# Five linear layers of a two-block transformer started two tiles at a time, with a chunked scratch layout and two gate buffers

## The chip, the cores and the metric

The kernel runs on one core of a Trainium2 chip, in one launch. The metric is the device time of that core in microseconds (us). Engines are called PE (matrix multiply), DVE (vector), ACT (activations), POOL (the general engine) and SP (which here only issues DMAs).

## What is computed

Two blocks on a sequence of 1024 tokens with 1024 features, in float32.

First block, once:

```python
h = h + hybrid_mixer(rmsnorm(h), ...)      # projection, gate z, conv, state space scan in 8 chunks of 128, pooling
h = h + memory_cross_attention(rmsnorm(h), rmsnorm(mem), ...)
h = h + swiglu(rmsnorm(h), ...)
x = rmsnorm(h)
```

In the state space part (16 heads of 64, 2 groups, state 128) each chunk of 128 tokens needs the running sum `a_cs` of every head along the tokens, spread over all partitions, for `exp(a_cs[l] - a_cs[s])`. The result is multiplied by `silu(z)`, z being the first 1024 columns of the input projection.

Second block, two layers: an even one (`proj` into a grouped attention with 8 heads, a latent attention with 8 heads, and a gate of 1024 columns), and an odd one (windowed attention with 16 heads and a sink, and a gate). Each is

```python
h = rms_norm(x, norm_w) * (1 + scale) + shift
y = (attention(h @ w_in) * silu(gate)) @ w_out
x = x + gate_mod * y
```

and a last `rms_norm`.

## The kernel before, in words

Activations lie with the features on the partitions: eight blocks k of 128 features by 1024 tokens. Every product is made of three: each float32 operand is split into a high half, rounded by ACT (`wh`, `XH`, `AH`, `RAWH`), and a low half, the rest, made by DVE (`wl`, `XL`, `AL`, `RAWL`). `pe_linear` (L280 to L308) is the linear layer: for each tile j of 128 output columns it runs over the eight k and issues six matmuls of 128x512 for each (three products, two halves of the tokens), which accumulate in one of four PSUM tiles `P` of 128x1024. In tile 0 it waits for block k by `ready(k)` just before that block's six matmuls; later tiles need no wait. A function in `between` runs on PE after the tile of that number.

Weights come by one list, `order`, of slabs of 1024x128 (512 KB). `sp_weights` (L230) loads slab i into `wf[i % 2]` once slab i-2's low half is made. `act_weights` (L242) rounds it into `wh[i % 2]` once PE has ended the tile of slab i-2; `dve_weights` (L251) makes `wl`. So the weights of tile 2 are split when tile 0 has ended. ACT and DVE do this at the head of their work on each tile (`act_tiles`, `dve_tiles`), and every engine works through its program in the order written.

A root mean square norm over the features goes: squares by ACT (L348), sums by DVE (L355), `pe_roots` (16 matmuls of one column, L364), the square root on ACT (L371), five short DVE steps and a diagonal (L394), `pe_spread` (4 matmuls, L402), and the copy out by ACT (L408).

The five layers that matter here:

- `z0`, five tiles of the gate z, at the start. ACT and DVE make the halves of block k of the raw input in turn. The roots of the first norm run after tile 0 and its spread after tile 1; DVE and ACT can start on the gate and on x1 only after that spread.
- `lq`, two tiles, at the start of the even layer. After tile 0 PE runs the spread `d1`. ACT copies it out, DVE scales the eight blocks of H by it (L1728), SP writes each to DRAM (`spill2`, L678), and only then issues the load of the weight slab of layer `ck` (L239). ACT's next weight split stands in its program ahead of the second tile's square, which the norm of `lq` needs.
- `eo`, eight tiles, the even layer's output. Blocks 0 to 3 of the attention result are gated already. For blocks 4 to 7 ACT makes the silu (L2370), DVE multiplies (L2327), ACT rounds (L2372), DVE makes the low half (L1300), one block after the other.
- `vo`, two tiles, at the start of the odd layer. DVE and ACT make the shifted norm block by block (L1697, L1687, L1701).
- `oo`, eight tiles, the odd layer's output. For each block DVE multiplies by the gate (L2727), ACT rounds (L2714), DVE makes the low half (L1300). The gates lie in four buffers `T`; gate j of 4 to 7 is loaded by SP when the low half of block j-4 is there (L2558).

The state space part: after the convolution layer, layer `z2` makes the last two gate tiles. `act_conv`'s `gate` (L727) puts silu of the tile in the one buffer `ZG` (L733) and ACT issues the store to `scratch_g` (L735); the second waits until the first store has landed. ACT's split of the weights of `so`, the layer after the scan, stands ahead of each of the two gates. PE's first transposes of the scan wait until both gates have left PSUM. ACT writes the running sums `[16 heads, 1024]` to the DRAM tensor `scratch_a` (L869). `sp_rows(n)` (L878) loads the 128 columns of chunk n from it, spread over all 128 partitions, 1 MB in SBUF: for each partition 16 pieces of 512 bytes, 4 KB apart in DRAM. SP issues chunks 0 to 3 in `sp_conv` after the weights of `z2`, chunk 4 and the gates' loads (L931) after `z2`, chunks 5 and 6 during the scan, and chunk 7 after the eight reloads of H. `act_decay(n)` (L1045, L1050) works on chunk n.

Of the kernel before, what the change touches and what calls it, by code (L numbers as in the profile page):

```python
# [7 lines left out]
F32 = mybir.dt.float32  # L8
# [111 lines left out]
class Kernel:  # L120
# [159 lines left out]
    def pe_linear(self, e, stage, xh, xl, ready, emptied, tokens=S, width=128, between=None, through=()):  # L280

        j = 0
        for n in range(self.count[stage][0]):
# [177 lines left out]
    def pe_z0(self, e):  # L461
# [4 lines left out]
                       lambda j: [(self.s.dve, ("z", j))], between=between)  # L466
# [225 lines left out]
    def act_conv(self, e):  # L692
# [34 lines left out]
        def gate(e, j):  # L727
            e.wait_ge(*self.s.mm.to(("z2", j)))
            if j:
                e.wait_ge(*self.s.g[6].to("out"))  # L730
            else:
                e.wait_ge(*self.s.act.to("dtx"))
            e.activation(sb["ZG"][:, :], self.tile("z2", j), ACT.Silu).then_inc(*self.s.act.up(("z", 6 + j)))  # L733
            e.wait_ge(*self.s.act.here())
            e.dma_start(self.dr["gT"][:, 6 + j, :], sb["ZG"][:, :]).then_inc(*self.s.g[6 + j].up("out"))  # L735
        self.act_tiles(e, "z2", gate)
# [26 lines left out]
    def sp_conv(self, e):  # L763
# [8 lines left out]
        self.sp_weights(e, self.no["so", 0])  # L772
        e.wait_ge(*self.s.dt.to("rows"))
        self.sp_rows(e, 0)
        self.sp_rows(e, 1)
# [86 lines left out]
    def act_dt_sums(self, e):  # L862
# [6 lines left out]
        e.dma_start(self.dr["aT"], rows).then_inc(*self.s.dt.up("rows"))  # L869
# [7 lines left out]
    def sp_rows(self, e, n):  # L877
        e.dma_start(self.rows_of(n)[:, :, :],  # L878
                    self.dr["aT"][:, 128 * n:128 * n + 128].partition_broadcast(128)).then_inc(*self.s.r[self.ROWS[n]].up(n))
# [207 lines left out]
    def dve_ssd(self, e):  # L1087
# [21 lines left out]
        for c in range(-1, 8):  # L1109
# [15 lines left out]
            if c > 0:  # L1125
# [3 lines left out]
                else:  # L1129
                    e.wait_ge(*s.g[7].to("out"))  # L1130
# [744 lines left out]
    def pe_even(self, e):  # L1875
        s = self.s

        def linear(stage, emptied, behind=None):
            self.pe_linear(e, stage, self.XH, self.XL, self.x4_ready, emptied, between=behind and {0: behind})
# [480 lines left out]
    def pe_even_out(self, e):  # L2360
        s = self.s
        self.pe_linear(e, "eo", self.AH, self.AL, lambda k: [(s.lo, ("eo", k))], lambda j: [(s.dve, ("h5", j))])
# [18 lines left out]
    def dve_even_out(self, e):  # L2381
        s = self.s
        for j in range(8):
            if j > 3:
                self.dve_gate(e, j)
# [27 lines left out]
    def pe_odd(self, e):  # L2413
        s = self.s
        ready = lambda k: [(s.lo, ("x5", k))]
        self.pe_linear(e, "vo", self.XH, self.XL, ready, lambda j: [(s.act, ("vo", j))])
# [288 lines left out]
    def pe_odd_out(self, e):  # L2705
        s = self.s
        self.pe_linear(e, "oo", self.XH, self.XL, lambda k: [(s.lo, ("oo", k))], lambda j: [(s.dve, ("h6", j))])
# [369 lines left out]
```

## Time and profile before

| | |
|---|---|
| median of 3 runs | 3194.72 us (3190.4 to 3196.64) |
| the profiled execution: its time | 3196.34 us |
| its span in the profile | 3194.5 us |
| PE busy | 2965.2 us, 93% of the span |
| DVE, ACT, POOL busy | 1694.7, 1262.5, 386.0 us |
| mean granted clock of PE | 0.967 of full speed |

The time of the execution is 1.84 us longer than the span, which is what lies around it. Matmul records overlap, since a matmul is pipelined: the start of one to the start of the next is what PE spends on it.

### The profile page before, as it was taken

The numbers are of one execution on the slowest core, as the hardware profiler recorded it, in microseconds if no ns is written. First come the engines' busy times: TensorE is split into PE (matmuls) and PEld (weight loads), VectorE is DVE, ScalarE is ACT, GpSimd is POOL, SyncE is SP. The second block draws the span as 40 slices with busy tenths as digits, with TensorE's granted clock in tenths as the row PEclk, the third lists the DMA queues.
The fourth block names the chain that finished last, engine by engine and source line by source line (L and its number), as shares of the span: only waits on it lengthen the run. The fifth ranks groups of instructions, "written<-read, shape, count | busy, mean of one in ns | idle before, by whom it ended". The sixth has DMA issues, their size and how long they took to land.

```text
span 3194.5 us, 38728 instructions
## 1 busy us (share of the span) xinstructions
PE 2965.2 (93%) x15570; PEld 2481.8 (78%) x15570; DVE 1694.7 (53%) x2101; ACT 1262.5 (40%) x2078; POOL 386.0 (12%) x224
## 2 busy tenths in 40 slices
PE   8999987899999999999999789889999889999987
PEld 6877865688988777888888567778888667879965
DVE  6563555654454444444344625688888634326653
ACT  5321445322343111111112325577767524427741
POOL 0000004200000000000000000255445100004410
PEclk9999998999999999999999899999999989999988
DMA  4112245112302222332331211100001221121031
GB/s 138 53 47 100 67 98 159 41 33 75 98 21 60 79 84 83 86 90 73 87 89 45 97 43 60 53 1 11 11 14 55 85 92 40 56 87 43 16 106 66
DMA packets 244528, 210.99 MB, mean 66 GB/s; under 512 B 9072, under 2 KB 219120, under 8 KB 243840
## 3 DMA queue, kind: packets, MB, share of 16 engines
q1 hardware_dynamic: 240864, 195.88, 20.9%
q10 hardware_dynamic: 3488, 12.65, 1.1%
q8 instruction: 125, 2.05, 0.3%
q14 instruction: 51, 0.42, 0.0%
HBM read 175.93 MB, written 30.47 MB: 65 GB/s over the span
## 4 chain that ended last, share of the span: by engine, by line
PE 81%; DVE 8%; ACT 5%; issue 2%; DMA 2%; POOL 2%; SPq 1%; DVEq 0%; ACTq 0%; POOLq 0%
PE P L300 59%; PE P L269 4%; PE P L2062 3%; PE P L272 2%; PE P L274 2%; PE P L273 2%; POOL T L2322 1%; PE P L2076 1%; DVE PTL L1300 1%; PE P L2075 1%; PE P L943 1%; DVE WST L2301 1%; PE P L402 1%; PE P L1332 1%; PE P L364 1%
## 5 line engine op out<-in xcount | busy, mean ns | idle before, releaser
L256 DVE TENSOR_TENSOR wl<-wf,wh 128x1024 fp32r<-128x1024 f32 (+4 forms) x239 | 251.7, 1053 | 1026.0 <-ACT wh L248 1025.8
L248 ACT ACTIVATE wh<-wf 128x1024 fp32r<-128x1024 f32 (+4 forms) x239 | 220.0, 921 | 1170.2 <-PE P L300 1047.5
L300 PE MATMUL P<-AQ,wh 128*128 128x512 f32 x1920 | 519.8, 393 | 13.1 <-DVE AQ L1300 10.6
L300 PE MATMUL P<-XH,wh 128*128 128x512 f32 (+1 forms) x1376 | 438.0, 400 | 46.1 <-DVE XL L1701 17.1
L2322 POOL TENSOR_TENSOR T<-T,WST 128x1024 f32<-128x1024 f32 x128 | 242.6, 1896 | 1668.9 <-DVE WST L2294 1668.9
L300 PEld LDWEIGHTS P<-AQ,wh 128*128 128x128 f32 x1920 | 362.5, 189 | 91.4 <-issue 10.4
L300 PE MATMUL P<-XL,wh 128*128 128x512 f32 (+1 forms) x1376 | 430.8, 395 | 0.0
L300 PE MATMUL P<-XH,wl 128*128 128x512 f32 (+1 forms) x1376 | 429.9, 394 | 0.0
L300 PEld LDWEIGHTS P<-XH,wh 128*128 128x128 f32 (+1 forms) x1376 | 258.3, 190 | 117.4 <-issue 40.1
L300 PEld LDWEIGHTS P<-XL,wh 128*128 128x128 f32 (+1 forms) x1376 | 260.5, 189 | 58.6
L300 PEld LDWEIGHTS P<-XH,wl 128*128 128x128 f32 (+1 forms) x1376 | 260.1, 189 | 58.1
L300 PE MATMUL P<-AQ,wl 128*128 128x512 f32 x960 | 297.7, 392 | 0.0
L300 PEld LDWEIGHTS P<-AQ,wl 128*128 128x128 f32 x960 | 181.7, 189 | 38.2
L300 PE MATMUL P<-FF,wh 128*128 128x512 f32 x704 | 193.0, 397 | 6.0 <-ACT wh L248 3.0
L1300 DVE TENSOR_TENSOR PTL<-P,PTH 128x512 fp32r<-128x512 f32 x256 | 164.5, 684 | 53.2 <-ACT PTH L2201 52.1
L269 PE MATMUL P<-consts,T 128*128 128x128 f32 x1112 | 146.5, 275 | 28.2 <-POOL T L2322 25.2
L2201 ACT ACTIVATE PTH<-P 128x512 fp32r<-128x512 f32 x256 | 139.1, 595 | 83.5 <-PE P L269 80.8
L300 PEld LDWEIGHTS P<-FF,wh 128*128 128x128 f32 x704 | 134.1, 192 | 36.6 <-ACT wh L248 6.0
L2301 DVE TENSOR_REDUCE WST<-P 128x1 f32<-128x1024 f32 x128 | 155.8, 1217 | 1.7 <-PE P L2062 1.6
L269 PEld LDWEIGHTS P<-consts,T 128*128 128x128 f32 x1112 | 124.3, 141 | 40.6 <-DVE PTL L1300 23.7
L2701 POOL TENSOR_TENSOR WS<-WS,WST 128x768 f32<-128x768 f32 (+1 forms) x64 | 87.3, 1363 | 466.7 <-DVE WST L2680 456.4
L2208 ACT ACTIVATE T<-P,WST 128x1024 f32<-128x1024 f32 x128 | 143.4, 1120 | 0.1
(379 smaller groups left out, 4926.4 us busy)
## 6 DMA issues: line engine op xcount, KB each, us to landing
AW<-ada_w SPq DMA_DIRECT2D x48, 512.0 KB, 3.7
wf<-w_gate_up SPq DMA_DIRECT2D x44, 512.0 KB, 4.9
wf<-w_in SPq DMA_DIRECT2D x28, 512.0 KB, 3.8
scratch_h<-H SPq DMA_DIRECT2D x24, 512.0 KB, 5.7
H<-scratch_h SPq DMA_DIRECT2D x24, 512.0 KB, 7.6
scratch_g<-T ACTq DMA_DIRECT2D x22, 512.0 KB, 3.2
wf<-odd_w_in SPq DMA_DIRECT2D x20, 512.0 KB, 3.7
wf<-even_w_in SPq DMA_DIRECT2D x17, 512.0 KB, 3.8
```

Source lines behind the costliest of these rows:

```text
L248: e.activation(self.sb["wh"][i % 2][:, 0:m], self.sb["wf"][i % 2][:, 0:m], ACT.Copy).then_inc(*self.s.w_hi.up(i))
L256: e.tensor_tensor(l, f, h.bitcast(F32), ALU.subtract).then_inc(*self.s.w_lo.up(i))
L269: return e.transpose(out, in_, self.sb["consts"][p0:p0 + n, a + p0:a + p0 + n])
L272: e.matmul(out, wh, xh, start=first, stop=False)
L300: ins = e.matmul(self.P[slot][0:m, t:t1], w, x[:, k, t:t1], start=first and k == 0, stop=last and k == kb - 1)
L1300: e.tensor_tensor(lo, src, hi.bitcast(F32), ALU.subtract).then_inc(*self.s.lo.up(name))
L2062: ins = e.matmul(p[:, ks], a[:, qs], c[:, ks], start=m == 0, stop=m == len(passes) - 1)
L2201: e.activation(self.probs("PTH", at, d), self.turned(d), ACT.Copy).then_inc(*s.hi.up(("pt", at, d)))
L2208: e.activation(self.px(at), self.P[at % 2], ACT.Exp, bias=w[:, 0:1], accum_out=w[:, 1:2]).then_inc(*s.act.up(("exp", at)))
L2301: e.tensor_reduce(sb["WST"][n % 4][:, 0:1], self.P[n % 2], AX, ALU.max, negate=True).then_inc(*s.dve.up(("max", n)))
L2322: e.tensor_tensor(self.px(n), self.px(n), r, ALU.mult).then_inc(*s.pool.up(("sc", n)))
L2701: e.tensor_tensor(x, x, r, ALU.mult).then_inc(*s.pool.up(("wsc", n)))
```

## The change

- `pe_first_pair` is new: tiles 0 and 1 of a layer are made side by side. For k from 0 to 5 the six matmuls of tile 0 are followed by those of tile 1; then tile 0's k 6 and 7, its signal and its `between`, then tile 1's. Both tiles' weights are waited for ahead of the first matmul. Layers `z0`, `lq`, `eo`, `vo` and `oo` use it.
- In `eo` the silu and the gating of block j+1 are put ahead of the halves of block j, on ACT and on DVE; in `oo` DVE's gating likewise.
- `ZG` becomes two buffers, the second at T + 4096, where the convolution's buffers were; the second gate waits for no store, and the split of a slab of `so` stands behind each gate. What waited for the second store in the scan (a write to T[3]) waits for the first one.
- `scratch_a` becomes `[8, 16, 128]`: the store is cut in pieces of 512 bytes, and the load of a chunk reads, for each partition, 8 KB in a run.
- SP issues the rows of chunk 0 ahead of the weight slabs of `z2`.

```diff
+    def pe_first_pair(self, e, stage, xh, xl, ready, emptied, between):
+        halves, slots = [], []
+        for j in range(2):
+            i = self.no[stage, j]
+            halves.append(tuple(self.halves(i)))
+            slots.append(self.tiles[stage, j][0])
+            e.wait_ge(*self.s.w_hi.to(i))
+            e.wait_ge(*self.s.w_lo.to(i))
+            self.pe_place(e, slots[j])
+        kb = self.order[self.no[stage, 0]].shape[1]
+        steps = [(j, k) for k in range(kb - 2) for j in range(2)] + [(j, k) for j in range(2) for k in (kb - 2, kb - 1)]
+        for j, k in steps:
+            if j == 0:
+                for count, key in ready(k):
+                    e.wait_ge(*count.to(key))
+            w1, w2 = (h[:, k, :] for h in halves[j])
+            for w, x, first, last in ((w1, xh, True, False), (w1, xl, False, False), (w2, xh, False, True)):
+                for t in (0, 512):
+                    ins = e.matmul(self.P[slots[j]][:, t:t + 512], w, x[:, k, t:t + 512], start=first and k == 0,
+                                   stop=last and k == kb - 1)
+            if k == kb - 1:
+                ins.then_inc(*self.s.mm.up((stage, j)))
+                self.emptied[slots[j]] = emptied(j)
+                if between and j in between:
+                    between[j](e)
...
@@ pe_linear
-        j = 0
-        for n in range(self.count[stage][0]):
+        j = 2 if paired else 0
+        if paired:
+            self.pe_first_pair(e, stage, xh, xl, ready, emptied, between)
+        for n in range(j, self.count[stage][0]):
...
@@ act_conv
         def gate(e, j):
             e.wait_ge(*self.s.mm.to(("z2", j)))
-            if j:
-                e.wait_ge(*self.s.g[6].to("out"))
-            else:
+            x = sb["ZG"][j][:, :]
+            if j == 0:
                 e.wait_ge(*self.s.act.to("dtx"))
-            e.activation(sb["ZG"][:, :], self.tile("z2", j), ACT.Silu).then_inc(*self.s.act.up(("z", 6 + j)))
+            e.activation(x, self.tile("z2", j), ACT.Silu).then_inc(*self.s.act.up(("z", 6 + j)))
             e.wait_ge(*self.s.act.here())
-            e.dma_start(self.dr["gT"][:, 6 + j, :], sb["ZG"][:, :]).then_inc(*self.s.g[6 + j].up("out"))
-        self.act_tiles(e, "z2", gate)
+            e.dma_start(self.dr["gT"][:, 6 + j, :], x).then_inc(*self.s.g[6 + j].up("out"))
+            self.act_weights(e, self.no["so", j])
+        for j in range(2):
+            gate(e, j)
@@ sp_conv
-        self.sp_weights(e, self.no["so", 0])
+        self.sp_weights(e, self.no["z2", 0])
         e.wait_ge(*self.s.dt.to("rows"))
         self.sp_rows(e, 0)
+        self.sp_weights(e, self.no["so", 0])
         self.sp_rows(e, 1)
@@ act_dt_sums, sp_rows
-        e.dma_start(self.dr["aT"], rows).then_inc(*self.s.dt.up("rows"))
+        e.dma_start(self.dr["aT"].rearrange("n h t -> h n t"),
+                    rows.rearrange("h (n t) -> h n t", n=8)).then_inc(*self.s.dt.up("rows"))
...
-                    self.dr["aT"][:, 128 * n:128 * n + 128].partition_broadcast(128)).then_inc(*self.s.r[self.ROWS[n]].up(n))
+                    self.dr["aT"][n].partition_broadcast(128)).then_inc(*self.s.r[self.ROWS[n]].up(n))
@@ dve_ssd
-                    e.wait_ge(*s.g[7].to("out"))
+                    e.wait_ge(*s.g[6].to("out"))
@@ act_even_out (dve_even_out has the same shift of dve_gate)
-            if j > 3:
-                e.wait_ge(*s.gl[j].to("back"))
-                e.activation(GA[:, j, :], GA[:, j, :], ACT.Silu).then_inc(*s.act.up(("gate", j)))
+            if 3 <= j < 7:
+                e.wait_ge(*s.gl[j + 1].to("back"))
+                e.activation(GA[:, j + 1, :], GA[:, j + 1, :], ACT.Silu).then_inc(*s.act.up(("gate", j + 1)))
@@ dve_odd_out
-        for j in range(8):
+        def gate(j):
             e.wait_ge(*s.gl[j].to("end"))
             e.tensor_tensor(T[j % 4], self.sb["O2"][j][:, :], T[j % 4], ALU.mult).then_inc(*s.dve.up(("o2", j)))
+        gate(0)
+        for j in range(8):
+            if j < 7:
+                gate(j + 1)
             self.dve_low(e, ("oo", j), self.XL[:, j, :], T[j % 4], self.XH[:, j, :])
...
-    sb["ZG"] = put("ZG", "T", 8256 + 4096, [128, 1024], F32)
+    sb["ZG"] = [put(f"ZG{i}", "T", (8256 + 4096, 4096)[i], [128, 1024], F32) for i in range(2)]
...
-    dr["aT"] = nc.dram_tensor("scratch_a", [16, S], F32, kind="Internal").ap()
+    dr["aT"] = nc.dram_tensor("scratch_a", [8, 16, 128], F32, kind="Internal").ap()
```

## Rows read from the trace of the kernel before

**Rows 1.** The page: busy time of each engine.

```profile
PE 2965.2 (93%) x15570; PEld 2481.8 (78%) x15570; DVE 1694.7 (53%) x2101; ACT 1262.5 (40%) x2078; POOL 386.0 (12%) x224
```

**Rows 2.** Timeline of `z0`: start, us, engine, line, out<-in, count [idle before].

```profile
12.12 2.05 PE L300 MATMUL P<-RAW,wh 128*128 128x512 f32 x4 [12.12 <-DVE RAW L449]
...
16.97 1.07 PE L300 MATMUL P<-RAW,wh 128*128 128x512 f32 x4
...
29.56 1.84 PE L364 MATMUL P<-consts,T 128*128 128x1 f32 x16
...
42.29 1.88 PE L402 MATMUL P<-T,consts 128*128 128x512 f32 x4
...
43.61 1.50 PE L300 MATMUL P<-RAW,wh 128*128 128x512 f32 x4
...
33.53 1.22 DVE L394 TENSOR_TENSOR T<-consts,RS 128x1024 f32<-128x1024 f32 x1
```

**Rows 3.** Timeline of `lq`, PE, DVE, SP and ACT.

```profile
1788.29 1.19 PE L300 MATMUL P<-XH,wh 128*128 128x512 f32 x2 [5.08 <-DVE XL L1701]
...
1806.17 1.88 PE L402 MATMUL P<-T,consts 128*128 128x512 f32 x4
...
1830.21 1.92 PE L364 MATMUL P<-consts,T 128*128 128x1 f32 x16 [0.35 <-DVE T L355]
...
1809.15 9.65 DVE L1728 SCALAR_TENSOR_TENSOR H<-H,vecs,T 128x1024 f32<-128x1024 f32 x8 [0.40 <-ACT T L408]
...
1819.20 13.47 SPq L239 DMA_DIRECT2D wf<-even_w_in  x4
...
1825.83 1.06 ACT L248 ACTIVATE wh<-wf 128x1024 fp32r<-128x1024 f32 x1 [5.96 <-DMA wf<-even_w_in]
```

**Rows 4.** Timeline of `eo`, PE and DVE.

```profile
2514.07 2.05 PE L300 MATMUL P<-AQ,wh 128*128 128x512 f32 x4 [6.38 <-DVE AQ L1300]
...
2542.95 1.07 PE L300 MATMUL P<-AQ,wh 128*128 128x512 f32 x4
...
2544.31 1.07 PE L300 MATMUL P<-AQ,wh 128*128 128x512 f32 x4
...
2523.08 1.23 DVE L1300 TENSOR_TENSOR AQ<-O,AQ 128x1024 fp32r<-128x1024 f32 x1 [1.13 <-ACT AQ L2372]
```

**Rows 5.** Timeline of `vo`, PE.

```profile
2632.22 1.19 PE L300 MATMUL P<-XH,wh 128*128 128x512 f32 x2 [5.03 <-DVE XL L1701]
...
2650.12 0.62 PE L300 MATMUL P<-XH,wh 128*128 128x512 f32 x2
```

**Rows 6.** `oo`: PE's timeline, and the landing time of the gates' loads (L2558).

```profile
3064.25 1.19 PE L300 MATMUL P<-XH,wh 128*128 128x512 f32 x2 [4.56 <-DVE XL L1300]
...
3090.05 0.62 PE L300 MATMUL P<-XH,wh 128*128 128x512 f32 x2
...
DMA to landing us min/median/max: 3.6/3.7/4.3
```

**Rows 7.** Timeline around `z2` and the scan's start, PE and ACT.

```profile
492.28 1.94 PE L269 MATMUL P<-consts,XS 128*128 128x128 f32 x8 [25.72 <-ACT ZG L733]
...
475.23 1.06 ACT L248 ACTIVATE wh<-wf 128x1024 fp32r<-128x1024 f32 x1 [16.84 <-DMA wf<-w_out_mix]
...
491.11 1.02 ACT L733 ACTIVATE ZG<-P 128x1024 f32<-128x1024 f32 x1 [12.38 <-DMA scratch_g<-ZG]
```

**Rows 8.** DMA views: 504 to 517 us, one chunk's rows alone; then 0 to 60.

```profile
DMA packets 2065, 1.07 MB, mean 82 GB/s; under 512 B 16, under 2 KB 2064, under 8 KB 2064
...
GB/s 0 164 328 303 328 407 401 421 412 412 410 360 294 251 7 0 0 0 0 0 0 0 200 159 1 0 0 0 0 0 48 298 277 355 71 0 0 0 0 0
```

**Rows 9.** The last chunk's rows: timeline of ACT, DVE and PE.

```profile
570.25 4.78 ACT L1045 ACTIVATE RM<-RM,AT 128x128 f32<-128x128 f32 x16 [11.17 <-DMA RM<-scratch_a]
...
576.15 2.35 DVE L1097 TENSOR_TENSOR RM<-RM,P 128x1024 f32<-128x1024 f32 x2 [3.08 <-ACT RM L1050]
...
580.82 1.98 PE L989 MATMUL P<-ST,BC 128*128 128x512 f32 x4 [2.84 <-DVE ST L1143]
```

More of the change, by code:

```diff
@@ L278, in tile, with pe_linear @@
         return self.P[slot][0:m, 0:tokens]
-    def pe_linear(self, e, stage, xh, xl, ready, emptied, tokens=S, width=128, between=None, through=()):
-        j = 0
-        for n in range(self.count[stage][0]):
+    def pe_first_pair(self, e, stage, xh, xl, ready, emptied, between):
[23 more added lines that the diff above has]
+                    between[j](e)
+    def pe_linear(self, e, stage, xh, xl, ready, emptied, tokens=S, width=128, between=None, paired=False,
+                  through=()):
+        j = 2 if paired else 0
+        if paired:
+            self.pe_first_pair(e, stage, xh, xl, ready, emptied, between)
+        for n in range(j, self.count[stage][0]):
             i = self.no[stage, n]
@@ L465, in pe_z0 @@
                        lambda k: [(self.s.hi, ("raw", k)), (self.s.lo, ("raw", k))],
-                       lambda j: [(self.s.dve, ("z", j))], between=between)
+                       lambda j: [(self.s.dve, ("z", j))], between=between, paired=True)
     def act_z0(self, e):
@@ L1878, in linear @@
         def linear(stage, emptied, behind=None):
-            self.pe_linear(e, stage, self.XH, self.XL, self.x4_ready, emptied, between=behind and {0: behind})
+            self.pe_linear(e, stage, self.XH, self.XL, self.x4_ready, emptied, between=behind and {0: behind},
+                           paired=stage == "lq")
         linear("lq", lambda j: [(s.act, ("lq", "sq", j))], lambda e: self.pe_spread(e, "d1", self.T[2]))
@@ L2361, in pe_even_out @@
         s = self.s
-        self.pe_linear(e, "eo", self.AH, self.AL, lambda k: [(s.lo, ("eo", k))], lambda j: [(s.dve, ("h5", j))])
+        self.pe_linear(e, "eo", self.AH, self.AL, lambda k: [(s.lo, ("eo", k))], lambda j: [(s.dve, ("h5", j))],
+                       paired=True)
         self.pe_rstd(e, "n5", self.T[2], s.dve.to(("n5", "sum", 7)))
@@ L2383, in dve_even_out @@
         for j in range(8):
-            if j > 3:
-                self.dve_gate(e, j)
+            if 3 <= j < 7:
+                self.dve_gate(e, j + 1)
             self.dve_low(e, ("eo", j), self.AL[:, j, :], self.sb["O"][:, j, :], self.AH[:, j, :])
@@ L2415, in pe_odd @@
         ready = lambda k: [(s.lo, ("x5", k))]
-        self.pe_linear(e, "vo", self.XH, self.XL, ready, lambda j: [(s.act, ("vo", j))])
+        self.pe_linear(e, "vo", self.XH, self.XL, ready, lambda j: [(s.act, ("vo", j))], paired=True)
         self.pe_linear(e, "ko", self.XH, self.XL, ready, lambda j: [(s.act, ("ko", j))])
@@ L2706, in pe_odd_out @@
         s = self.s
-        self.pe_linear(e, "oo", self.XH, self.XL, lambda k: [(s.lo, ("oo", k))], lambda j: [(s.dve, ("h6", j))])
+        self.pe_linear(e, "oo", self.XH, self.XL, lambda k: [(s.lo, ("oo", k))], lambda j: [(s.dve, ("h6", j))],
+                       paired=True)
         self.pe_rstd(e, "n6", self.T[2], s.dve.to(("n6", "sum", 7)))
```

## The prediction, made before the changed kernel was run

> **What bounds the kernel now.** I read the page first: PE is busy for 2965.2 of 3194.5 us [rows 1], so a gain can only come from the 229 us in which PE stands still, or from stretches in which its clock is low. The list of PE's waits was next, then the timeline around each place that the diff touches. The reader is to see two kinds of stall. One is a single large one: PE ends `z2` and then stands for 25.72 us until ACT has copied out the last gate tile [rows 7]. The others lie in tile 0 of a layer whose input is made block by block: PE has six matmuls for a block and then waits for the next. What PE does at full clock is seen in tile 1 of `eo`, where the last two blocks start at 2542.95 and 2544.31 [rows 4]: 1.36 us for a block of six matmuls, so 0.2267 for one, 10.88 for a tile, 21.76 for a pair. After a long idle it is slower: in `z0` the first 12 matmuls took 16.97 - 12.12 = 4.85 us [rows 2] instead of 2.72, mostly at the lower of the clock's two levels (1.2 and 2.4 GHz). So a start costs 2.13 us more, and I charge that to every pair.
>
> **What the pairs do.** Nothing is computed more or less. A pair has 2.72 us of PE work per block where tile 0 had 1.36. DVE makes a block's input in two operations of 1.2 to 1.3 us, less than 2.72 where nothing else holds it, so PE becomes the bound, and the pair ends 21.76 + 2.13 = 23.89 us after its start.
>
> - **`vo`.** Start 2632.22, end 2656.1. Before, tile 1 began at 2650.12 [rows 5] and ended 10.88 later, at 2661.0. Gain 4.9.
> - **`eo`.** Start 2514.07, end 2538.0. Before, tile 1's last block began at 2544.31 [rows 4] and ended at 2545.7. Gain 7.7. This holds if the halves keep up. The low half of a block takes 1.23 us, and DVE stood 1.13 us before it, waiting for ACT [rows 4]: DVE's gating and ACT's rounding of one block ran one after the other. With the gating one block ahead, DVE has two operations of about 1.2 us a block and no wait, 2.35 us, below PE's 2.72.
> - **`oo`.** Start 3064.25, end 3088.1. Before, tile 1 began at 3090.05 [rows 6] and ended at 3100.9. Gain 12.8. It is the largest since tile 0 took 25.8 us here for 48 matmuls. The gating one ahead now stands in DVE's program in front of a low half, so a late gate load would hold the block before it. Load j starts when the low half of j-4 is done, and DVE has four operations, some 4.7 us, before it needs it; it lands in 3.6 to 4.3 us [rows 6]. That is hidden, with 0.4 to spare; if it is not, PE has 0.4 us a block in hand.
> - **`z0`.** Here tile 0 ends later: 84 matmuls (14 blocks) and 2.13 us after 12.12, at 33.3, where it ended at 29.56. The roots run then, and the diagonal was ready 33.53 + 1.22 - 29.56 = 5.19 us after their start [rows 2]. Tile 1's last two blocks (2.72) are too little to cover that, so PE waits for it at 38.5 and the spread of 43.61 - 42.29 = 1.32 us ends at 40.0 instead of 43.61. Everything behind hangs on the spread. Gain 3.6, not the 9 that the pair as such would give.
> - **`lq`.** This one should lose. The spread `d1` stands behind tile 0. It began at 1806.17; now it begins 19.04 + 2.13 us after 1788.29, at 1809.5 [rows 3], 3.3 later. ACT's copy, DVE's eight operations of 9.65 us, SP's spills and, behind them on SP's queue, the slab load issued at 1819.20 all hang on it. ACT then split that slab after a wait of 5.96 us for the load, at 1825.83, and the second square of `lq` stands behind that split, and PE's roots at 1830.21 behind that. Tile 1 ends earlier, but PE only waits longer before the roots. Loss 3.3. Below: 0, if the load is found not to be last. Above: 5, if the roots run at the lower clock after the longer wait.
>
> In all five the weights of tile 2 are split when tile 0 has ended: one ACT operation of 1.06 and one DVE operation of 1.23, 2.3 us with little between, and PE has 2.72 us of tile 1 left. The cover is 0.3 us at most; gone, it costs what is missing, once a layer. I take 0.
>
> **The scan.** ACT's program held the split of the first `so` slab ahead of the gate, and it waited 16.84 us for that slab's load, until 475.23; then the second gate waited 12.38 us for the first one's store, until 491.11 [rows 7]. Both loads and store stood in queues behind the rows of chunks 0 to 3. With two buffers the first gate waits for its tile alone, and the second for the end of `z2`, 492.28 - 25.72 = 466.56 [rows 7]. ACT's 1.02 us and some 0.2 for the two signals give PE's start at 467.8 instead of 492.28. Gain 24.5. PE is then not idle before: its eight transposes took 1.94 us at the lower level [rows 7], half of that at the higher one; gain 1.0, between 0 and 1.9.
>
> This needs the first `so` slab by 466. SP's program now has rows 0 before the slabs of `z2`, some 12 us earlier, and the same rows 1, 2 and 3 before `so`. **The rows' cost** is what the trace does not show in the new form. One chunk alone took some 13 us, 1 MB at 82 GB/s in pieces under 2 KB [rows 8]. Bounds: the same rate, and the 400 to 421 GB/s at which the input's pieces of 4 KB came [rows 8], 2.6 us. I take the fast end, since the new pieces are in one run like those; but all partitions read the same 8 KB, which no row shows, so the slow end stays open. The Trainium skill ("DMA: Bandwidth & Descriptors", Specifications) gives 512 bytes as the least transfer for line rate, and by it the old pieces would be large enough and the new ones no faster; the trace disagrees for the old ones, which ran at a fifth of the rate of the others. By that rule the sum would be the first rival's.
>
> The **last chunk's rows** were late: ACT waited 11.17 us for them, until 570.25, DVE 3.08 for ACT, and PE 2.84 for DVE [rows 9]. They are issued at the same point as before. If they land 6 us earlier, none of these waits is left; gain 2.8, and 0 if the rate is the old one. The store of `scratch_a` in 128 pieces instead of 16 moves 64 KB and has some 12 us until SP reaches it; cost 0. Reading g[6] instead of g[7] takes a wait off DVE that was over anyway; 0. Scan together: 24.5 + 1.0 + 2.8 = 28.3. ACT's decays, which bound the first chunks, only move.
>
> **Sum.** 3.6 + 28.3 - 3.3 + 7.7 + 4.9 + 12.8 = 54.0 us. Between these places PE is the bound, or (in the attention) work that only moves, so the gains add. Against the profiled execution's 3196.34 us this is 3142.3; the median of the runs is 1.6 lower, so I say 3142.
>
> **Rivals.**
> - *The rows are no faster* (12%). For: the same-address reads, and the rule above. Then the last chunk's wait stays, 2.8. If the first `so` slab still lands at 475.2, ACT's second gate stands behind it and PE starts at 477.5, 9.7 later; but rows 0 has left the queue 12 us ahead, which speaks for no such loss. 3145 to 3155, likeliest 3147.
> - *`lq` loses nothing* (8%): the load lands in time whatever the spread does. ACT's 5.96 us wait for it speaks against that. 3139.
> - *The weights of tile 2 are late* (7%), by some 1 us in each of four layers, the cover being 0.3. 3146.
> - *The clock* (3%), the one on the other side. The pair changes the PSUM tile with every six matmuls; if PE does not come to the higher level in it, 12 matmuls cost 4.85 throughout. Then each pair of 96 takes 38.8 instead of 23.9 us, three times 14.9 more, and `z0`'s and `lq`'s 84 take 12.8 more each: 70.3 us, 3212, slower by 17. It decides from 54 us on, that is if about 11 of the 15 us come in each of the five. Against: before, PE rose within 5 us of every steady start. The Trainium skill ("TensorE: Matmul & The Clock Gate", A second HAM failure mode) tells of a kernel whose clock swung since it cycled through PSUM banks with short idles between. No row here shows that for pairs.
> - The forecast itself has 68%, and 2% is left for what I don't see.
>
> **How the numbers follow.** Within the forecast the cold start may cost nothing or twice as much in each pair: 10.7 us either way, 3132 to 3153. The rows' slow end reaches 3155, the `lq` rival lies inside. Range 3131 to 3156. About 0.2% (6 us) is what a measurement of this kernel can tell from no change. Faster has all but the clock and half of the unseen: 0.96; same 0.01; slower 0.03.
>
> **What the new profile would show.** PE's wait for `ZG` near 467 gone or under 2 us; the rows' loads landing in 3 to 5 us; ACT's wait at L1045 gone; in `eo`, `vo` and `oo` no waits of PE for low halves after the first block; in `z0` a wait of about 1 us before the spread; in `lq` a longer wait before the roots. I am wrong if `z0` gains the full 9 us or `lq` gains, if rows land after 12 us, or if the clock column shows low levels inside the pairs.

## The result, and the profile after

The changed kernel takes 3141.61 us (median of 4 runs, 3140.52 to 3146.3), against 3193.23 us (3190.4 to 3196.64) for the kernel before beside it: a ratio of 0.9841, 95% interval 0.9824 to 0.9858, so 51.6 us faster. The forecast said 3142. By the profiled executions it is less close: that of the changed kernel took 3146.3 us, with a span of 3144.5, so the spans differ by 50.0 us where the sum of the forecast had 54.0. That the median fell on the forecast is thus partly luck, and the terms are judged by the traces.

Lines of the changed kernel's code that come up below: L300 is the pair's matmul, L331 that of later tiles, L395 the roots, L433 a spread, L763 the gate's `ZG`, L912 the rows' load, L1079 the decay, L1762 the scaling of x0, L1334 a low half. First the page, and rows of PE's list of waits (who waited for what; us in total, times, longest):

```profile
PE 2956.3 (94%) x15570; PEld 2482.8 (79%) x15570; DVE 1694.3 (54%) x2101; ACT 1261.3 (40%) x2078; POOL 385.7 (12%) x224
```

```profile
PE P L395 <- DVE T L386: 17.3, 3, 7.4
PE P L300 <- DVE RAW L480: 12.2, 1, 12.2
PE P L300 <- DVE XL L1735: 10.1, 2, 5.1
...
PE P L300 <- DVE AQ L1334: 6.4, 1, 6.4
...
PE P L300 <- DVE XL L1334: 4.6, 1, 4.6
...
PE P L269 <- ACT ZG L763: 1.2, 1, 1.2
```

PE's work is the same [rows 1]. L300 is in the pairs alone, and its waits for input are one at each pair's start (1, 2, 1 and 1 times, five in all) and none inside a pair. The wait for the last gate is 1.2 us instead of 25.72 [rows 7]. One wait has grown: the roots, up to 7.4 us at a time.

The gain, stretch by stretch. Each is from one PE row to another in both traces, so the rows add up to the difference of the spans.

| stretch | before | after | gain | forecast |
|---|---|---|---|---|
| start to the first tile behind `z0`'s spread | 43.61 | 40.81 | 2.8 | 3.6 |
| to the end of `z2` | 422.95 | 424.19 | -1.2 | 0 |
| to the first matmul of `so` (the scan) | 128.53 | 100.30 | 28.2 | 28.3 |
| to the first of `lq` | 1193.20 | 1191.12 | 2.1 | 0 |
| to the first behind `lq` and `ck` | 67.23 | 72.78 | -5.6 | -3.3 |
| to the first of `eo` | 658.55 | 659.07 | -0.5 | 0 |
| `eo` to its roots | 103.14 | 95.63 | 7.5 | 7.7 |
| to the first of `vo` | 15.01 | 15.01 | 0.0 | 0 |
| `vo` to the first of `ko` | 28.8 | 23.38 | 5.4 | 4.9 |
| to the first of `oo` | 403.25 | 404.30 | -1.1 | 0 |
| the pair of `oo` | 36.68 | 24.50 | 12.2 | 12.8 |
| to the end of the span | 93.6 | 93.4 | 0.2 | 0 |

**The scan.** ACT's timeline (start, us, line, tile) around the two gates, and PE's first transposes:

```profile
456.74 1.01 ACT L763 ACTIVATE ZG<-P 128x1024 f32<-128x1024 f32 x1
...
458.22 1.06 ACT L248 ACTIVATE wh<-wf 128x1024 fp32r<-128x1024 f32 x1 [0.48 <-ACT ZG L763]
465.04 1.02 ACT L763 ACTIVATE ZG<-P 128x1024 f32<-128x1024 f32 x1 [5.76 <-PE P L331]
...
466.21 1.06 PE L269 MATMUL P<-consts,XS 128*128 128x128 f32 x8 [1.21 <-ACT ZG L763]
```

The split of the `so` slab has no DMA to wait for (16.84 us before), the second gate waits for PE's tile only, and the transposes run at the higher clock, 1.06 us instead of 1.94 [rows 7]. The rows' loads (line L912, DMA view) land in a third of the time; before, the middle one took 17.7 us:

```profile
DMA to landing us min/median/max: 4.4/5.1/8.1
```

**`lq`.** PE, with DVE's and ACT's rows that hold it up:

```profile
1756.42 1.19 PE L300 MATMUL P<-XH,wh 128*128 128x512 f32 x2 [5.08 <-DVE XL L1735]
...
1778.38 1.88 PE L433 MATMUL P<-T,consts 128*128 128x512 f32 x4
...
1801.29 3.54 PE L395 MATMUL P<-consts,T 128*128 128x1 f32 x16 [7.38 <-DVE T L386]
...
1781.36 9.65 DVE L1762 SCALAR_TENSOR_TENSOR H<-H,vecs,T 128x1024 f32<-128x1024 f32 x8 [0.40 <-ACT T L439]
...
1796.92 1.06 ACT L248 ACTIVATE wh<-wf 128x1024 fp32r<-128x1024 f32 x1 [4.84 <-DMA wf<-even_w_in]
```

The spread comes 21.96 us after the first matmul instead of 17.88 [rows 3], 4.1 us later. The slab's load takes part of that back, since ACT waits 4.84 us for it instead of 5.96: the roots start 44.87 us after the first matmul instead of 41.92, 3.0 later. After 7.38 us of idle instead of 0.35 they take 3.54 us instead of 1.92, and the tile behind them, still partly at the lower clock, takes 13.56 us (1804.70 to 1818.26) instead of 12.59 (1831.99 to 1844.58). That is 3.0 + 1.6 + 1.0 = 5.6 us.

**`z0` and `oo`.** In `z0` PE now waits a little for the diagonal, as the forecast had it. In `oo` the pair runs without a stop; DVE waits once for a gate's load, and PE does not notice:

```profile
34.14 1.84 PE L395 MATMUL P<-consts,T 128*128 128x1 f32 x16
...
39.39 1.98 PE L433 MATMUL P<-T,consts 128*128 128x512 f32 x4 [0.53 <-DVE T L425]
40.81 1.49 PE L331 MATMUL P<-RAW,wh 128*128 128x512 f32 x4
...
3026.59 1.19 PE L300 MATMUL P<-XH,wh 128*128 128x512 f32 x2 [4.57 <-DVE XL L1334]
...
3051.09 0.66 PE L331 MATMUL P<-XH,wh 128*128 128x512 f32 x2
...
3039.34 1.22 DVE L2765 TENSOR_TENSOR T<-O,T 128x1024 f32<-128x1024 f32 x1 [1.41 <-DMA T<-scratch_g]
```

### The profile page after: what moved, and what is told of

It is laid out like the page before. It is cut to its first block, busy times and chain, and to the rows that moved or that the text cites. A ratio compares the mean times of both kernels' runs of the same rounds, so it can differ in the third digit from the quotient of the medians.

```text
span 3144.5 us, 38727 instructions
## 1 busy us (share of the span) xinstructions
PE 2956.3 (94%) x15570; PEld 2482.8 (79%) x15570; DVE 1694.3 (54%) x2101; ACT 1261.3 (40%) x2078; POOL 385.7 (12%) x224
## 4 chain that ended last, share of the span: by engine, by line
PE 85%; DVE 6%; ACT 3%; issue 2%; POOL 2%; DMA 1%; SPq 0%; DVEq 0%; ACTq 0%; POOLq 0%
PE P L331 59%; PE P L269 4%; PE P L300 4%; PE P L2097 3%; PE P L272 2%; PE P L274 2%; PE P L273 2%; POOL T L2357 2%; PE P L2111 1%; PE P L977 1%; DVE PTL L1334 1%; PE P L2110 1%; PE P L433 1%; DVE WST L2336 1%; PE P L1366 1%
## 5 line engine op out<-in xcount | busy, mean ns | idle before, releaser
L331 PE MATMUL P<-AQ,wh 128*128 128x512 f32 x1856 | 498.9, 391 | 2.6 <-issue 2.6
L331 PE MATMUL P<-XH,wh 128*128 128x512 f32 (+2 forms) x1280 | 402.2, 396 | 17.3 <-ACT T L379 9.1
L331 PEld LDWEIGHTS P<-AQ,wh 128*128 128x128 f32 x1856 | 348.6, 188 | 76.3 <-issue 4.1
L331 PE MATMUL P<-XL,wh 128*128 128x512 f32 (+2 forms) x1280 | 398.2, 393 | 0.0
L331 PE MATMUL P<-XH,wl 128*128 128x512 f32 (+2 forms) x1280 | 397.7, 392 | 0.0
L331 PEld LDWEIGHTS P<-XH,wh 128*128 128x128 f32 (+2 forms) x1280 | 239.8, 188 | 74.8 <-issue 22.8
L331 PE MATMUL P<-AQ,wl 128*128 128x512 f32 x928 | 286.6, 390 | 0.0
L331 PEld LDWEIGHTS P<-XH,wl 128*128 128x128 f32 (+2 forms) x1280 | 240.5, 188 | 53.5
L331 PEld LDWEIGHTS P<-XL,wh 128*128 128x128 f32 (+2 forms) x1280 | 240.3, 188 | 53.7
L331 PEld LDWEIGHTS P<-AQ,wl 128*128 128x128 f32 x928 | 174.5, 188 | 36.6
L331 PE MATMUL P<-FF,wh 128*128 128x512 f32 x704 | 192.9, 397 | 6.7 <-ACT wh L248 3.6
L1334 DVE TENSOR_TENSOR PTL<-P,PTH 128x512 fp32r<-128x512 f32 x256 | 164.6, 684 | 53.5 <-ACT PTH L2236 52.4
L269 PE MATMUL P<-consts,T 128*128 128x128 f32 x1112 | 146.2, 275 | 28.3 <-POOL T L2357 25.4
L331 PEld LDWEIGHTS P<-FF,wh 128*128 128x128 f32 x704 | 134.2, 192 | 37.4 <-ACT wh L248 6.7
```

Of the source, the lines that this page charges most:

```text
L269: return e.transpose(out, in_, self.sb["consts"][p0:p0 + n, a + p0:a + p0 + n])
L331: ins = e.matmul(self.P[slot][0:m, t:t1], w, x[:, k, t:t1], start=first and k == 0, stop=last and k == kb - 1)
L1334: e.tensor_tensor(lo, src, hi.bitcast(F32), ALU.subtract).then_inc(*self.s.lo.up(name))
```

## Experiments

Ten kernels ran. Each is given with its ratio to the kernel before, run beside it on the same chip (medians 3193.2 to 3198.2 in the four sessions), and with the stretch of the trace that the edit touches. Some 6 us is what a median can tell; the stretches are finer, about 0.1 us where the rows in them have the same clock. Of the variants of the changed kernel all but e5, e7 and e8 lie within 6 us of it, so what is said of them rests on the stretches.

### 1 and 2: which edit emptied the scan's wait?

The forecast gave 24.5 us to the two gate buffers. The rival owner is the scratch layout. Each is put alone into the kernel before.

```diff
e1: kernel before, and only
-        e.dma_start(self.dr["aT"], rows)
+        e.dma_start(self.dr["aT"].rearrange("n h t -> h n t"), rows.rearrange("h (n t) -> h n t", n=8))
...
-        self.dr["aT"][:, 128 * n:128 * n + 128].partition_broadcast(128)
+        self.dr["aT"][n].partition_broadcast(128)
...
-    dr["aT"] = nc.dram_tensor("scratch_a", [16, S], F32, kind="Internal").ap()
+    dr["aT"] = nc.dram_tensor("scratch_a", [8, 16, 128], F32, kind="Internal").ap()
e2: kernel before, and only the change's act_conv gate, ZG in two buffers, and dve_ssd's wait for g[6]
```

> The kernel before with the new layout of the scratch tensor and nothing else: one gate buffer, the old order on ACT and SP, no pairs. Theory (the clogged queue is the cause): a chunk's rows land in about 5 us instead of 14 to 28, so the first slab of so is there before ACT asks for it and the store of the first gate lands in about 4 us, before z2 ends. The stall of 25.7 us ahead of the scan falls under 2 us and the last chunk's wait of 11 us is gone: some 28 us faster than the kernel before, about 3165, without a second buffer. Rival (the single buffer is the cause, as my forecast told it): the second gate still waits several us for the store; a gain of 2.8 us for the last chunk and part of the 24.5.

> The kernel before with two gate buffers and the split of the so slabs behind each gate, but the old layout, the old order of SP, no pairs. Theory (the clogged queue): ACT's split of the first so slab still waits for the load until about 475, now behind the first gate and ahead of the second, so the second gate comes at about 476 and PE starts the scan at about 477.5 instead of 492.3: 12 to 15 us faster, 3179 to 3182, and the last chunk's wait of 11 us on ACT stays. Rival (the buffer alone frees it): PE starts at 468 and the kernel is 24 us faster, about 3170.

Layout alone: 3165.41 us, ratio 0.9904 (0.9890 to 0.9919). Buffers alone: 3180.44 us, 0.9952 (0.9937 to 0.9966). First the timeline of the kernel with the layout alone, ACT and PE:

```profile
460.43 1.04 ACT L248 ACTIVATE wh<-wf 128x1024 fp32r<-128x1024 f32 x1
461.38 1.01 ACT L733 ACTIVATE ZG<-P 128x1024 f32<-128x1024 f32 x1
...
469.77 1.00 ACT L733 ACTIVATE ZG<-P 128x1024 f32<-128x1024 f32 x1
...
470.92 1.07 PE L269 MATMUL P<-consts,XS 128*128 128x128 f32 x8 [2.21 <-ACT ZG L733]
```

And with the buffers alone:

```profile
457.87 1.01 ACT L732 ACTIVATE ZG<-P 128x1024 f32<-128x1024 f32 x1
...
476.44 1.06 ACT L248 ACTIVATE wh<-wf 128x1024 fp32r<-128x1024 f32 x1 [17.56 <-DMA wf<-w_out_mix]
477.40 1.00 ACT L732 ACTIVATE ZG<-P 128x1024 f32<-128x1024 f32 x1
```

From the end of `z2` to `so` the kernel before takes 128.53 us, the one with the layout 101.56, the one with the buffers 114.86, the changed one 100.30. So the layout alone brings 27.0 of the 28.2 us, and the buffers 13.7 alone but only 1.3 on top of it. (The kernel called "buffers alone" also has the weight splits moved behind the gates, and in the 1.3 are besides SP's new place for the rows of chunk 0 and the pairs; these runs don't part them.) With one buffer the second gate no longer waits for the first one's store, because that store is no longer in a queue behind slow rows; PE's 2.21 us there are the gate standing behind a weight split, which the change also moved. With two buffers and slow rows ACT stands for the `so` slab instead, and the second gate stands behind it.

### 3: the old layout in the changed kernel

```diff
e8: changed kernel, with the store, the load and the shape of scratch_a as before
```

> The changed kernel with the scratch tensor laid out as before; buffers, order and pairs stay. Theory (the clogged queue): the rows take 12 us each again. The first slab of so comes about 12 us sooner than before the change, since the rows of chunk 0 left the queue earlier, so PE's start of the scan moves little, but the last chunk's wait of 11 us on ACT is back and the second slab of so may hold ACT's first decay: 3 to 6 us slower, about 3146. Rival (the slab still comes at 475): the stall ahead of the scan is back by 10 us, 3155.

3151.4 us, 0.9869 (0.9853 to 0.9886). The stretch from `z2` to `so` is 110.96 us, 10.7 longer than with the new layout. That is more than the 3 to 6 us that I expected, although the rival's condition did not come (the `so` slab still at 475). It is also 3.9 shorter than with the buffers alone: here SP issues the rows of chunk 0 ahead of the weight slabs of `z2`, at 412.62 instead of 428.75, and ACT has the first `so` slab at 464.88 instead of 476.44. Most of the loss is at the other end of the scan, and its size is what the expectation missed. ACT and PE there:

```profile
542.88 4.79 ACT L1078 ACTIVATE RM<-RM,AT 128x128 f32<-128x128 f32 x16 [11.41 <-DMA RM<-scratch_a]
...
553.46 3.78 PE L1022 MATMUL P<-ST,BC 128*128 128x512 f32 x4 [3.09 <-DVE ST L1176]
...
566.99 1.97 PE L269 MATMUL P<-consts,T 128*128 128x128 f32 x8 [1.32 <-DVE XS L1136]
```

The wait for the last chunk's rows is as long as before [rows 9], and PE's stall 3.09 us against 2.84. But behind it the four matmuls take 3.78 us instead of 1.98, and the transposes 1.97 instead of 1.09. PE's clock in that stretch, from the windows (us, busy times by engine, PEclk, DMA share, GB/s):

```profile
555.00:560.00 5.00, 5.00 (x18) 3.63 (x16) 1.23 (x1) 0.00 (x0) 1.96 (x1) 0.50 0.00 0
560.00:565.00 5.00, 5.00 (x25) 5.00 (x25) 1.00 (x1) 0.00 (x0) 0.00 (x0) 0.50 0.00 0
```

From the last chunk's first transposes (of `XS`) to `so` it is 33.2 us here (540.96 to 574.18), 26.5 in the kernel before, 28.2 with the buffers alone, and 24.1 in the changed kernel and with the layout alone. So nearly the same stall cost 2.4 us (2.84 us long, in the kernel before), 4.1 (2.99, buffers alone) and 9.1 (3.09, here). The four matmuls behind it took 1.98, 3.51 and 3.78 us. The granted clock stayed at 1.00 in the first, was at 0.50 for some 3 us in the second, and in the third for all of the 12 us that PE then worked without a stop (553.46 to 565.67).

### 4 to 7: who makes `lq` slower, and can it be turned round?

```diff
e3: changed kernel, lq without the pair
-                           paired=stage == "lq")
+                           paired=False)
e4: changed kernel, the slab issued ahead of the spills
+        self.sp_weights(e, self.no["ck", 0] + 1)
         self.sp_spill(e, "spill2", lambda j: [(self.s.dve, ("x0", j))])
e10: changed kernel, the spread d1 ahead of lq instead of behind tile 0, on PE and ACT, and DVE's scaling in two halves
+        self.pe_spread(e, "d1", self.T[2])
-        linear("lq", ..., lambda e: self.pe_spread(e, "d1", self.T[2]))
+        linear("lq", ...)
...
+        self.act_first_norm(e)
-        self.act_tiles(e, "lq", ..., {0: self.act_first_norm})
+        self.act_tiles(e, "lq", ...)
...
+        self.dve_first_norm(e, range(4))
-        self.dve_tiles(e, "lq", ..., {0: self.dve_first_norm})
+        self.dve_tiles(e, "lq", ..., {0: lambda e: self.dve_first_norm(e, range(4, 8))})
e5: both, e4 and e10
```

> The changed kernel, with layer lq made one tile after the other again. Theory: the pair in lq delays the spread d1 by 4.1 us and so the first norm, the spill, the slab load behind it and the roots; undone, the span from the first matmul of lq to the first of the gate layer falls from 72.8 us to about 67.2 and the kernel is 4 to 6 us faster than the changed one, about 3136. Rival (only the clock's phase differs): the stretch stays within 2 us of 72.8 and the time at 3141.

> The changed kernel, with SP's load of the slab of ck issued ahead of the eight spills instead of behind them; lq stays a pair. Theory (the chain in lq runs through the spills and the load): ACT's wait of 4.84 us for the load goes, the roots come 4 to 5 us earlier, and since PE then stands idle for about 3 us only, part of the low clock goes too: 5 to 7 us faster than the changed kernel, about 3135. Rival (the square, which waits for the first norm, is last anyway): under 1 us.

> The changed kernel with d1's spread ahead of lq and half of x0's scaling ahead of the second square, but the slab of ck loaded behind the spills as in the changed kernel. Theory (two separate gains: the spread ahead frees the spill and the slab early and keeps PE at the high clock at the start of the pair; the slab ahead of the spills is worth little once x0 is ready early): the slab is issued near 1780 instead of 1791, roots near 1789, so lq's stretch from its first matmul to the next layer's is 60 us where the kernel with both edits has 57 and the changed one 72.8; time about 3128.5. Rival (only the slab's place matters, and the spread's place adds nothing without it): stretch 70 us or more, time 3138 to 3142.

> The changed kernel with the slab of ck loaded ahead of the spills, and the spread d1 taken out of the pair and run before it, in PE's idle time ahead of the first block; ACT copies it out before the layer, and DVE makes four blocks of the first norm before it splits the weights of va and four after. Theory (in lq it is the place of the spread that costs, not the pair): PE stands only for its first block and the squares of ck, and the stretch from lq's first matmul to the gate layer's falls from 72.8 us (64.2 in the run with the slab ahead) to about 61; about 11 to 12 us faster than the changed kernel, 3130. Rival (the halves of va come late, or the spread delays the pair's first block at the low clock): the stretch stays at 63 us or more.

Where the spread goes ahead of `lq`, that layer's start moves too, so the stretch here runs from the spread before it (four matmuls out of `ACC`, 8.86 us ahead of `lq` in the changed kernel) to the first matmul behind `lq` and `ck`:

| kernel | stretch | median | ratio (95%) |
|---|---|---|---|
| before | 76.10 | | |
| changed | 81.64 | 3141.61 | 0.9841 (0.9824 to 0.9858) |
| `lq` unpaired (e3) | 76.09 | 3136.27 | 0.9814 (0.9799 to 0.9828) |
| slab ahead (e4) | 73.11 | 3135.99 | 0.9811 (0.9795 to 0.9827) |
| spread ahead (e10) | 73.27 | 3135.95 | 0.9814 (0.9801 to 0.9828) |
| both (e5) | 65.80 | 3125.4 | 0.9788 (0.9773 to 0.9803) |

Without the pair the stretch is what it was before, to 0.01 us: the pair in `lq` is the whole of that loss. In that kernel ACT waits 5.91 us for the slab and PE 0.30 us ahead of the roots, against 5.96 and 0.35 before [rows 3]. Each of the two repairs gives 8.4 to 8.5 us and both 15.8. For the spread alone neither theory nor rival came true: from the first matmul of `lq` it takes 64.4 us, between the 60 and the 70 of the two, and the time is 3135.95 and not 3128.5. The slab's place is not worth little once the spread is early; it gives another 7.5 us. For both edits the expectation was too low, 61 us and 3130 against 56.9 and 3125.4. Rows of the spread-only kernel, ACT and PE:

```profile
1787.70 1.06 ACT L248 ACTIVATE wh<-wf 128x1024 fp32r<-128x1024 f32 x1 [5.16 <-DMA wf<-even_w_in]
...
1792.08 3.54 PE L395 MATMUL P<-consts,T 128*128 128x1 f32 x16 [4.12 <-DVE T L386]
```

The slab still holds ACT for 5.16 us, and the roots come late (1792.08 where 1789 was expected) and at the low clock. With both edits, PE and ACT:

```profile
1748.69 1.96 PE L433 MATMUL P<-T,consts 128*128 128x512 f32 x4 [1.20 <-ACT T L439]
1752.57 0.70 PE L300 MATMUL P<-XH,wh 128*128 128x512 f32 x2 [1.92 <-DVE XL L1735]
...
1785.83 1.84 PE L395 MATMUL P<-consts,T 128*128 128x1 f32 x16
...
1780.50 1.05 ACT L248 ACTIVATE wh<-wf 128x1024 fp32r<-128x1024 f32 x1
```

The split waits for nothing, the roots follow the second tile at once and at the higher clock, and there is a second gain, which the expectation for this kernel did not have (that for the spread alone, written later, did): the spread fills part of the idle before the pair (1.92 us left of 5.08), and the pair's first two matmuls take 0.70 us instead of 1.19, so it has no cold start. What the spread's place and the halving of DVE's scaling give apart from each other was not tried. The version with both beats both kernels of the comparison, by 16 us the changed one.

### 8 and 9: pairs and early gating in the output layers

```diff
e6: changed kernel, the gating of eo and oo back behind the halves (act_even_out, dve_even_out, dve_odd_out as before); pairs stay
e7: changed kernel, eo and oo without pairs; early gating stays
```

> The changed kernel with the gating of eo and oo put back behind the block before it; the pairs stay. Theory: in oo the blocks then come every 3.48 us, slower than the pair's 2.72, so the pair ends about 28.5 us after its start instead of 24.5; in eo four blocks are ready at the start, the pair takes 24 us of PE's time and all blocks are there by then, so nothing changes. 3 to 5 us slower than the changed kernel, about 3145, all in oo. Rival (the gating ahead is what brings the gain in both): 8 us or more, also in eo.

> The changed kernel with eo and oo one tile after the other, the gating ahead kept. Theory: tile 0 is bound by its inputs, one each 2.3 us, and tile 1 comes whole behind it: the first two tiles take about 28.5 us in oo and 25 to 26 in eo instead of 24.5 and 24. 5 to 8 us slower than the changed kernel, about 3148. Rival (the pair as such brings nothing once the inputs are fast): within 2 us.

| kernel | median | ratio (95%) | `eo` to its roots | `oo` to its roots |
|---|---|---|---|---|
| before | | | 103.14 | 105.93 |
| early gating alone (e7) | 3149.17 | 0.9857 (0.9842 to 0.9872) | 96.54 | 98.33 |
| pairs alone (e6) | 3147.54 | 0.9853 (0.9839 to 0.9868) | 95.63 | 97.85 |
| both (changed) | 3141.61 | 0.9841 (0.9824 to 0.9858) | 95.63 | 93.84 |

Both kernels keep the change's other edits. In `eo` the pair alone gives all 7.5 us and the early gating nothing on top of it; the early gating alone gives 6.6. In `oo` they give 7.6 and 8.1 alone and 12.1 together. DVE and PE in `oo` of the kernel with pairs alone:

```profile
3043.52 1.23 DVE L1334 TENSOR_TENSOR XL<-T,XH 128x1024 fp32r<-128x1024 f32 x1 [1.13 <-ACT XH L2751]
...
3047.01 1.23 DVE L1334 TENSOR_TENSOR XL<-T,XH 128x1024 fp32r<-128x1024 f32 x1 [1.13 <-ACT XH L2751]
...
3048.29 0.73 PE L300 MATMUL P<-XH,wh 128*128 128x512 f32 x2 [0.47 <-DVE XL L1334]
3051.77 0.74 PE L300 MATMUL P<-XH,wh 128*128 128x512 f32 x2 [1.83 <-DVE XL L1334]
```

A block takes DVE 3.49 us (3043.52 to 3047.01), 0.77 more than the pair's 2.72, since it waits 1.13 for ACT's rounding. Over four gated blocks that is 3.1 us, and `eo` has four blocks gated beforehand, a lead that covers it; `oo` has to gate all eight.

### 10: `z0` without the pair

```diff
-                       lambda j: [(self.s.dve, ("z", j))], between=between, paired=True)
+                       lambda j: [(self.s.dve, ("z", j))], between=between)
```

> The changed kernel with z0 alone back to one tile at a time; all else stays. Theory (the pair lets z0's spread come 2.8 us earlier, at 39.4 instead of 42.3, because tile 0 ends later and the roots and the diagonal are no longer hidden): the next tile starts at 43.6 as in the kernel before, and the time is 2.8 us above the changed kernel's 3141.6, about 3144.4. Rival (the 2.8 us are given back behind z0, for ACT and DVE set the pace of the next stage): the time stays at 3141.6 though the spread is late.

3145.38 us, 0.9845 (0.9831 to 0.9858). PE:

```profile
12.56 2.04 PE L331 MATMUL P<-RAW,wh 128*128 128x512 f32 x4 [12.56 <-DVE RAW L480]
...
30.00 1.84 PE L395 MATMUL P<-consts,T 128*128 128x1 f32 x16
...
44.00 1.49 PE L331 MATMUL P<-RAW,wh 128*128 128x512 f32 x4
```

From the first matmul to the first tile behind the spread 31.44 us, against 28.65 with the pair: 2.8. The delay is still there at the scan, whose first transposes start at 469.41 instead of 466.21 (0.4 of the 3.2 is the later start), so nothing between `z0` and the scan takes it back. The medians differ by 3.8 us between two sessions, which says no more than that it fits.

## Why the prediction was right, and where its steps were not

Each point has the forecast first and what was measured second.

- **The scan, 28.3 against 28.2.** (Its last term, the last chunk's wait, was 2.4 and not 2.8.) The size was right and the owner wrong. The step that fails is "with two buffers the first gate waits for its tile alone, and the second for the end of `z2`": that takes the `so` slab as landed, and with the buffers alone ACT waited 17.56 us for just that. The forecast names the condition ("This needs the first `so` slab by 466") and still books the 24.5 to the buffers. The same rows [rows 7] name both waits (a slab's load, a store), and both were transfers queued behind the rows of chunks 0 to 3, as the forecast says in the sentence ahead of that step. The layout frees both. The sum did not suffer, as both edits were in the change; a reader who had kept only the buffers would have had half. The rival that the rows are no faster had 3147 as its likeliest time; the measured cost of the old layout gives 3151.4, because it took the last chunk's wait at 2.8 us and it cost 9.1, most of it at the lower clock.
- **The rows' landing, "3 to 5 us" against 4.4 to 8.1.** The fast end was taken, and it held well enough: none comes after 12, and ACT no longer waits for them. PE's wait in the last chunk is 0.44 us instead of 2.84. The Trainium skill ("DMA: Bandwidth & Descriptors", Specifications) names 512 bytes as enough for the line rate. Here pieces of 512 bytes moved at 82 GB/s [rows 8], and it does not tell the two layouts apart. But the forecast was wrong to say that the trace disagrees on the size. A slab of `w_q` also comes in 1024 pieces of 512 bytes, out of rows 4 KB apart, each read once. Alone on the queues, from 662 to 667 us in the kernel before, it rose to 356 GB/s and landed in 3.6 us:

```profile
GB/s 0 0 0 0 0 0 0 0 0 0 0 0 4 156 61 61 176 295 266 299 279 291 328 352 348 344 356 291 205 82 0 0 0 0 0 0 0 0 0 0
DMA packets 1040, 0.52 MB, mean 105 GB/s; under 512 B 16, under 2 KB 1040, under 8 KB 1040
...
wf<-w_q SPq DMA_DIRECT2D x1, 512.0 KB, 3.6
```

  So the size of a piece alone is not what slows the rows, and since the new layout is read by all 128 partitions too, neither is the repeated reading alone. It is small pieces together with the repeated reading, or with the 4 KB from one piece to the next within a partition (512 KB in the slab's); which of the two no run here separates.
- **`lq`, -3.3 against -5.6.** The mechanism was right, and the unpaired kernel shows that it is all of the loss. Mis-sized: the spread's delay is 4.1 and not 3.3, since the cold start costs 84 matmuls 21.96 - 19.04 = 2.9 us and not 2.13. Of the 4.1 only 3.0 reach the roots, as ACT waits 1.1 us less for the slab. The roots cost 1.6 more at the lower clock and the tile behind them 1.0; I had named the first as the upper bound's reason and left it out of the sum, the second nowhere, and 5 was too small a bound.
- **`z0`, 3.6 against 2.8.** The same 2.9 us cold start: the roots begin 21.98 us after the first matmul, and I had 21.2. The rest, the diagonal that hides no longer, came as worked out. The sum has a slip of 0.2: 38.5 and 1.32 are 39.8, not 40.0, so its own terms give 3.8. "Not the 9 that the pair as such would give" has no row behind it and should not have stood there: the two tiles end at 38.9 (the spread's start less its wait of 0.53 us) instead of 42.29 [rows 2].
- **`eo`, 7.7 against 7.5.** The forecast hung the gain on the early gating ("this holds if the halves keep up"). It holds without. The step that failed looked at one block's rate and not at the lead of four blocks.
- **`oo`, 12.8 against 12.2, and `vo`, 4.9 against 5.4.** Right. In `oo` the pair took 24.50 us, a cold start of 2.7, and in `vo` 23.38, one of 1.6. The gate loads landed in 3.6 to 6.0 us, past the 4.7 that I had DVE need them in; the one wait of 1.41 us was inside PE's reserve, as the forecast had it for that case. The pairs-alone kernel shows that here the early gating earns 4.0 us.
- **Tile 2's weights.** Costed at 0, with 0.3 us of cover. No wait of PE for weights stands behind any of the pairs; in `oo` tile 2 follows 24.50 us after the start with no idle before it.
- **The clock rival.** Refuted: of the `oo` pair, the windows below (us, then busy times by engine, PEclk, DMA share, GB/s) have the lower level in the first 5 us and the higher one in nearly all of the other 20.

```profile
3026.00:3031.00 5.00, 4.42 (x11) 3.48 (x12) 5.00 (x6) 2.43 (x3) 0.00 (x0) 0.50 0.60 167
3031.00:3051.00 20.00, 20.00 (x87) 16.37 (x85) 11.75 (x11) 5.31 (x5) 0.00 (x0) 0.97 0.39 118
```

  One of the reasons that the forecast gave against this rival does not hold, though: it says that before, PE rose within 5 us of every steady start. In that trace the matmuls that begin at 1218.60 us reached the higher level only some 6 us after their start; from 1221 on (PE alone, in the same order) PE was never idle and the clock had a mean of 0.62:

```profile
1221.00:1226.00 5.00, 5.00 (x16) 0.62 0.42 101
```

- **What the sum left out.** Stretches in which nothing was edited (in the second only SP's order) moved by +2.1, -1.2, -1.1 and -0.5 us. Together they are -0.7, again some luck. For the most part the clock is what differs: added up over windows of 5 us, length times what the granted clock lacks to 1 is 2.7 us less in the first, 0.8 more in the third and 0.2 more in the fourth, and in the second the clock fell to 0.66 from 430 to 435 us where before it stayed at 1.00, and PE stood 0.47 us at 406. They also move between the experiments: the kernel with the layout alone has 29.2 us less span, of which the scan is 27.0.

## What to carry to other kernels

When two waits end in transfers, look first at what those transfers queue behind: one fast load did more here than a second buffer, and the buffer, with the weight splits moved behind the gates, was worth 13.7 us alone and, SP's order and the pairs included, 1.3 behind it. Two tiles side by side turn a layer's slow start into full work, but they end tile 0 later, so before pairing look for what hangs on tile 0 (here a norm's spread, a spill and a slab load), and move it ahead or out of the queue; that turned a loss of 5.6 us into a gain of 10.3. A remedy for a slow producer is worth its rate times the blocks that have no lead, so count the blocks that are ready when the layer starts.

## What the runs showed of the hardware

- **The same short stall has several prices.** About 3 us of waiting at the same place of the scan cost 2.4, 4.1 or 9.1 us, by how long the granted clock was at 0.50 behind it: not at all, some 3 us, or all of the 12 us of PE's work that followed. What decides it these runs do not show. In the roots of `lq`, 0.35 us of idle left 16 small matmuls at 1.92 us and 7.38 us made them 3.54.
- **Unchanged code moves by a microsecond or two with the clock.** The first four matmuls of one layer (the one that reads `FF`), in the kernel before and in the one with spread and slab ahead; the idle before is the same there, 0.7 us ahead of a group of 16 single-column matmuls:

```profile
1216.51 2.22 PE L1494 MATMUL P<-consts,AA 128*128 128x1 f32 x16 [0.72 <-DVE AA L1487]
1218.60 2.05 PE L300 MATMUL P<-FF,wh 128*128 128x512 f32 x4
```

```profile
1183.20 1.92 PE L1528 MATMUL P<-consts,AA 128*128 128x1 f32 x16 [0.73 <-DVE AA L1521]
1184.98 1.17 PE L331 MATMUL P<-FF,wh 128*128 128x512 f32 x4
```

  This start is cold in one and warm in the other, and from these roots to the next 16 single-column matmuls the first takes 130.9 us and the second 128.5. What decides it these runs do not show. Differences of that size between kernels say nothing of an edit elsewhere.
- **A few matmuls in the idle before a layer take its cold start away.** With four spread matmuls 1.92 us ahead of the pair its first two took 0.70 us and not 1.19; the same pair after 5.08 us of idle lost 2.9 us. In the kernel with the spread alone the four ran at the lower clock themselves (3.75 us instead of 1.96), and the pair behind them, with no idle between, began at 0.70 too. Whether filler work would do the same elsewhere was not tried.
- **A load that each of the 128 partitions repeats depends on how its 8 KB lie in DRAM.** 16 pieces of 512 bytes, 4 KB apart: one such load alone on the queues moved at 82 GB/s, and the eight landed in 17.7 us (median). With 8 KB in a run they landed in 5.1. Pieces of 512 bytes that are each read once are not slow: a weight slab of 1024 of them rose to 356 GB/s and landed in 3.6 us. The store of the sums in 128 pieces instead of 16 landed in the same 1.9 us.
